# Gate stage of a two-block network: experts in products of 512 columns with halves added, half the low parts on GpSimd, one-hot rows by a comparison and a multiplication

## The reference

```python
top_s, top_pos = lax.top_k(cand_s, PEER_TOPK)
e = jnp.take_along_axis(cand_i, top_pos, axis=-1)
g = jax.nn.softmax(top_s, axis=-1).astype(xc.dtype)
a = jax.nn.gelu(jnp.einsum("td,thkd->thk", xc, w_down[e]))
return jnp.einsum("thk,thkd->td", g * a, w_up[e])
```

## Time and profile before

| | |
|---|---|
| median of 3 runs | 1985.24 us (1984.35 to 1985.85) |
| profiled execution, its own time | 1986.74 us |
| its span | 1984.9 us |
| TensorE busy | 1894.7 us, 95% |
| VectorE busy | 1416.2 us, 71% |
| ScalarE busy | 992.2 us, 50% |
| GpSimd busy | 257.3 us, 13% |
| chain that ended last | PE 77%, DVE 11%, ACT 3% |

### The profile page before, as it was taken

One profiled execution on the slowest core, in us unless ns is written; L12 is line 12 of the kernel. 1 busy time (PEld: TensorE's weight loads), 2 busy tenths in 40 slices (PEclk: granted clock), 3 DMA queues, 4 the chain that ended last, 5 costly groups with the idle time before them and its releaser, 6 DMA issues.

```text
span 1984.9 us, 32618 instructions
## 1 busy us (share of the span) xinstructions
PE 1894.7 (95%) x12858; PEld 1725.7 (87%) x12858; DVE 1416.2 (71%) x2574; ACT 992.2 (50%) x1442; POOL 257.3 (13%) x118
## 2 busy tenths in 40 slices
PE   6889899999988999999999899999999999999998
PEld 6887799999968799999998899999988888888886
DVE  5897775558957773338567559988878887777776
ACT  6555544455435554455555455566653334444444
POOL 0001044440001034430000066000000000000000
PEclk9999999999998999999999999999999999999999
DMA  8654477766564255545435354577766765555452
GB/s 323 240 191 142 150 246 255 265 213 204 179 230 141 109 182 190 191 170 197 166 132 170 108 172 167 181 216 216 219 211 251 301 236 227 194 219 205 171 206 112
DMA packets 94551, 391.92 MB, mean 197 GB/s; under 512 B 7680, under 2 KB 41776, under 8 KB 56000
## 3 DMA queue, kind: packets, MB, share of 16 engines
q1 hardware_dynamic: 94112, 389.58, 55.7%
q10 hardware_dynamic: 288, 0.26, 0.1%
HBM read 371.72 MB, written 15.73 MB: 195 GB/s over the span
## 4 chain that ended last, share of the span: by engine, by line
PE 77%; DVE 11%; ACT 3%; issue 2%; DMA 1%; POOL 0%; ACTq 0%; DVEq 0%; SPq 0%
PE acc L566 9%; PE acc L568 9%; PE acc L567 9%; PE ps L570 8%; PE ps L572 7%; PE ps L571 7%; PE ps L582 5%; PE acc L570 3%; PE acc L571 3%; PE acc L572 3%; PE ps L583 3%; DVE wlo L1361 2%; PE ps L1316 1%; PE acc L1316 1%; DVE arena L1390 1%
## 5 line engine op out<-in xcount | busy, mean ns | idle before, releaser
L2433 ACT ACTIVATE whi<-raw 128x1024 fp32r<-128x1024 f32 x557 | 588.4, 1059 | 443.0 <-PE acc L568 219.5
L1361 DVE TENSOR_TENSOR wlo<-raw,whi 128x1024 fp32r<-128x1024 f32 x461 | 569.5, 1242 | 309.1 <-ACT whi L2433 305.8
L570 PE MATMUL ps<-hpair,whi 128*128 128x256 f32 x1400 | 400.8, 286 | 7.2 <-DVE wlo L1361 3.4
L572 PE MATMUL ps<-hpair,wlo 128*128 128x256 f32 x1400 | 396.0, 283 | 0.0
L571 PE MATMUL ps<-hpair,whi 128*128 128x256 f32 x1400 | 396.0, 283 | 0.0
L1361 POOL TENSOR_TENSOR wlo<-raw,whi 128x1024 fp32r<-128x1024 f32 x96 | 239.9, 2502 | 616.0 <-ACT whi L2433 615.7
L566 PE MATMUL acc<-whi,chi 128*128 128x512 f32 x752 | 296.9, 395 | 3.5 <-DVE wlo L1361 1.9
L568 PE MATMUL acc<-wlo,chi 128*128 128x512 f32 x752 | 294.4, 391 | 0.0
L567 PE MATMUL acc<-whi,clo 128*128 128x512 f32 x752 | 293.9, 391 | 0.0
L570 PEld LDWEIGHTS ps<-hpair,whi 128*128 128x128 f32 x1400 | 268.4, 192 | 10.8 <-issue 4.1
L571 PEld LDWEIGHTS ps<-hpair,whi 128*128 128x128 f32 x1400 | 268.5, 192 | 0.6
(11 more groups left out here) (457 smaller groups left out, 2863.4 us busy)
## 6 DMA issues: line engine op xcount, KB each, us to landing
raw<-in_peer_down SPq DMA_DIRECT2D x64, 1024.0 KB, 4.9
raw<-in_peer_up SPq DMA_DIRECT2D x64, 1024.0 KB, 5.0
arena<-in_ada SPq DMA_DIRECT2D x80, 512.0 KB, 4.9
raw<-in_w_gate SPq DMA_DIRECT2D x22, 1024.0 KB, 4.7
raw<-in_w_up SPq DMA_DIRECT2D x22, 1024.0 KB, 4.8
raw<-in_w_down SPq DMA_DIRECT2D x22, 1024.0 KB, 4.8
arena<-spill SPq DMA_DIRECT2D x14, 1024.0 KB, 6.8
spill<-hT_t SPq DMA_DIRECT2D x22, 448.0 KB, 6.1
```

The source lines that it names most:

```text
L570: e.matmul(out, hi, xh, start=start, stop=False, skip_group_check=True)
L572: i = e.matmul(out, lo, xh, start=False, stop=stop, skip_group_check=True)
L1361: e.tensor_tensor(out=lo, in0=w, in1=hi.bitcast(F32), op=ALU.subtract).then_inc(*X(("lo", j)))
L2433: e.activation(hi, w, ACT.Copy, scale=1.0).then_inc(*self.A(("hi", j)))
```

## The change

1. Experts 21 to 71 use `pe_mm2`. VectorE adds the halves of expert i - 1 at the end of turn i, ScalarE takes their Gelu in place, behind the copies of the gate steps of turn i - 1. For expert 71 both stand in the expert stage.
2. The low parts of peer_down blocks 21 to 71 go to GpSimd where the number is odd and stay on VectorE where it is even.
3. The four instructions for `oh1` become a comparison of 512 columns (iota, repeated for four tokens, with the tokens' keys, each repeated 128 times) and, behind a wait for it, a multiplication in place by the gates, repeated likewise.

```diff
@@ lo_engine
+        if name == "peer_down" and STEP0 <= 2 * i + half < NST:
+            return ("V", "G")[half]
         if name[:5] == "peer_":
             return "V" if j >= self.block_no["peer_down", VLO0 // 2, VLO0 % 2] else "G"
@@ pe_expert_down
-        if i >= NST:
+        if i >= STEP0:
             for k in range(8):
                 self.pe_mm2(e, ps, self.W.tile(e, "peer_down", 8 * i + k), k, *([("full", "expert", i)] if k == 7 else []))
             return
@@ ve_gates
             for n in steps(i):
                 self.ve_one_hots(e, n)
             self.ve_cuts(e, "peer_down", 8 * i + 7)
+            if i > STEP0:
+                self.ve_expert_halves(e, i - 1)
@@ ve_one_hots
-        for i in range(4):
-            t = 4 * n + i
-            e.tensor_scalar(out=m.oh1[:, n % 3, i * 128:(i + 1) * 128], in0=m.iota, scalar1=m.pk[:, 0, t:t + 1],
-                            scalar2=m.pg[:, t:t + 1], op0=ALU.is_equal, op1=ALU.mult).then_inc(
-                                *V(*([("oh1", n)] if i == 3 else [])))
+        one = m.oh1[:, n % 3, :].rearrange("p (t n) -> p t n", t=4)
+        e.tensor_tensor(out=one, in0=bc(m.iota.unsqueeze(1), [128, 4, 128]),
+                        in1=bc(m.pk[:, 0, 4 * n:4 * n + 4].unsqueeze(2), [128, 4, 128]), op=ALU.is_equal).then_inc(*V())
+        e.wait_ge(*V.last)
+        e.tensor_tensor(out=one, in0=one, in1=bc(m.pg[:, 4 * n:4 * n + 4].unsqueeze(2), [128, 4, 128]), op=ALU.mult).then_inc(
+            *V(("oh1", n)))
@@ ve_experts
         self.ve_weigh(e, 0)
+        self.ve_expert_halves(e, NST - 1)
@@ se_gates
         for i in range(STEP0, NST):
-            self.se_expert_down(e, i)
-            for n in steps(i):
...
+            self.se_cuts(e, "peer_down", 8 * i + 7)
+            if i > STEP0:
+                for n in steps(i - 1):
+                    self.se_gates_out(e, n)
+                self.se_gelu(e, i - 1)
@@ se_experts
             if i + 1 >= NST and i < 127:
-                self.se_expert_down(e, i + 1)
+                self.se_cuts(e, "peer_down", 8 * (i + 1) + 7)
+                if i + 1 == NST:
+                    self.se_gelu(e, NST - 1)
+                self.se_gelu(e, i + 1)
```

More of the change, by code:

```diff
@@ L2972, in se_expert_down, with se_gelu, se_gates_out @@
         self.se_cuts(e, "peer_down", 8 * i + 7)
[L2973 to L2977, removed]
         e.wait_ge(*self.at("full", "expert", i))
-        if i == NPRE + 16:
-            e.wait_ge(*self.at("end", "picked", "P"))
         e.activation(m.ge_t[i], self.banks.tile("expert", i)[:, 0:T], ACT.Gelu_apprx_tanh, scale=1.0).then_inc(
             *self.A(("out", "expert", i), ("gelu", i)))
+    def se_gelu(self, e, i):
+        x = self.m.ge_t[i] if i < NST else self.m.co[:, i % 2, :]
+        e.wait_ge(*self.at("out", "expert", i))
+        e.activation(x, x, ACT.Gelu_apprx_tanh, scale=1.0).then_inc(*self.A(("gelu", i)))
     def se_gates(self, e):
-        m, A = self.m, self.A
         for i in range(STEP0, NST):
-            self.se_expert_down(e, i)
-            for n in steps(i):
[L2989 to L2996, removed]
+            self.se_cuts(e, "peer_down", 8 * i + 7)
[3 more added lines that the diff above has]
+                self.se_gelu(e, i - 1)
+    def se_gates_out(self, e, n):
+        m = self.m
+        k, c = n // 2 % 3, n // 6
+        st = m.stage[k].rearrange("p (n t) -> p n t", t=8)[:, :, 4 * (n % 2):4 * (n % 2) + 4]
+        e.wait_ge(*self.at("full", "gates", n))
+        if c and n % 2 == 0:
+            e.wait_ge(self.spilled[k], 16 * c)
+            e.wait_ge(self.kept, 16 * (n // 2 - 2))
+        e.activation(st.rearrange("p n t -> p t n"), self.banks.tile("gates", n)[:, :].rearrange("p (t n) -> p t n", t=4),
+                     ACT.Copy, scale=1.0).then_inc(*self.A(("out", "gates", n)))
     def se_experts(self, e):
```

## The result

The changed kernel takes **2021.12 us** (median of 5 runs, 2020.05 to 2022.99); the kernel before, run beside it, 1984.86 (5 runs, 1983.99 to 1985.85). The ratio is 1.0181, with a 95% interval of 1.0167 to 1.0195: slower by 36 us, where 2025 was forecast. The profiled execution took 2020.05 us, with a span of 2018.3 and a mean granted clock of 0.989.

A forecast was written before the change was run, and what follows sets the result against it. TensorE was taken to bound the stage, VectorE after the change: exclusion 36, way in 1.5 and 1, way out 0.4 less 0.2, Gelu 1.4, sum +40 on 1985.24 us, so 2025 us, range 2010 to 2042.

The forecast's parts named there:

- The bound and its exchange: Stretch 1262 to 1458 us: TensorE alone sets the pace before; after the change TensorE waits for VectorE's one-hot rows.
- Idle some 35 us: Sign in the new profile: TensorE idle that long between experts and gate steps, waiting for one-hot rows.
- The exclusion: Expert and gate-step stage: GpSimd's low parts and VectorE work with two SBUF sources exclude each other; +36 us (30 to 45).
- A step of VectorE: One gate step's one-hot work on VectorE: 1.97 us with the new pair, 0.34 more than 1.63; bounds 1.8 to 2.15.
- a hold: Each GpSimd low part adds some 2.3 us to VectorE's chain, less 0.65 if a reduction lies under it.
- A: Rival: the exclusion doesn't reach the one-hot instructions' repeated operands; -1.7 us, 1983.5 us; chance 0.09.
- B: Rival: no exclusion, but the one-hot pair is dearer, 2.15 us a step; +3 to +7, 1990 us; chance 0.04.
- C: Rival: no exclusion, and 512-column products go faster, 2.72 us an expert; -6, 1979 us; chance 0.03.
- The way in: Route's end and first gate step: block 21's low part on GpSimd costs 1.5 us, late first rows about 1.
- The way out: After the last gate steps: +0.4 us before expert 0's weighing, -0.2 for experts 69 to 71 without gate steps.
- Gelu 71: Expert stage: the later Gelu delays expert 71's weighing and peer_up 71's low part; +1.4 us once.
- Moved copies: ScalarE copies gate steps out of PSUM behind the next high part: costed at nothing, since no high part waits for a transfer.

The follow-up runs named there:

- fourth experiment: The changed kernel, with keys and gates of the one-hot operations read from the PSUM banks the transposes leave them in: 1986.1 us, ratio 1.0011.
- seventh: The kernel before with the one-hot pair (comparison and multiplication) alone: 1986.2 us, ratio 1.0005.
- eighth experiment: The kernel before with only the 512-column products, added halves and moved copies, Gelu of expert 71 taken early: 1982.55 us, ratio 0.9982.
- sixth: The kernel before with the one-hot pair and the odd low parts on GpSimd, old products: 2013.6 us, ratio 1.0143.
- tenth: The kernel before with one-hot pair, odd low parts on GpSimd, and ScalarE's gate copies moved behind the next expert's high parts: 1999.3 us, ratio 1.0069.
- fifth experiment: The kernel before with only the odd low parts of blocks 21 to 71 on GpSimd: 1991.8 us, ratio 1.0031.
- ninth experiment: The changed kernel with the low parts of experts 21 and 23 left on VectorE: 2017.9 us, ratio 1.0172.

## Why the prediction was right, and where its sizes were off

**The bound and its exchange: right.** TensorE set the pace before, VectorE does after, TensorE's idle time stands before the one-hot rows. "Idle some 35 us" was too much: the waits for one-hot rows are 22.6 us in the whole stage, and in the stretch of 196 us TensorE is idle for 196.00 - 176.19 = 19.8, or 2.8 per period of 27.8. The period is 3.8 over TensorE's 24.0; of the other 1.0, some 0.7 is work that the clock stretched (4.7 us in seven periods, below), and the rest is not taken apart.

**The exclusion: right in kind, oversized.** Forecast +36 (30 to 45), measured +26.9, which lies below the range; the period is 27.8, just under the 28.1 that was the lower bound. Three terms were each a little dear. A step of VectorE is 1.92 instead of 1.97, -0.4 per period. A reduction is 0.60 instead of 0.65, -0.3. And a hold was put at 2.3, with one reduction beside a low part "only by chance" (28.9 in the middle). In the trace a hold adds 2.17, because the held instruction's own 0.68 is work that was due anyway, and two of three low parts regularly begin ahead of a reduction: 5.4 for three instead of the 5.8 that 28.9 contained. That work which reads PSUM is not held rested on one row, 0.69 under GpSimd; the fourth experiment shows it for three lines of operations, 192 instructions in all, with GpSimd's low parts beside them.

**The rivals.** A said that repeated operands might not count: comparisons with two repeated sources took up to 2855 ns, so they do. The section of the Trainium skill named there ("SBUF — State Buffer", "SBUF: two separate sides"), by which A doesn't happen, agrees with the trace in this too. B had the price in the pair: a step is 1.92, not 2.15, and the fourth kernel, with pair and low parts, keeps to TensorE's 24.0. (That the pair alone costs nothing that can be measured, 1.0005 [0.9994, 1.0016] in the seventh, doesn't decide it: even at 2.15 a step VectorE's 24.0 would fit in 24.4 there.) C had faster long products: with a gate step at 0.89, as the prediction counts it, an expert takes 2.78 to 2.83 in the stage, where 2.81 was taken and C had 2.72.

**The way in: undersized.** 2.5 forecast, 5.7 measured. Of the two cases for the predicated copy, held or not, I took the middle, and the copy is held for full, 1.9. The first one-hot rows cost 2.5, not 1: I had counted the wait behind the low part of block 23 as mostly hidden. And 1.3 is the clock's, which no term had.

**The way out:** +0.4 - 0.2 forecast, 0.6 measured from the last gate steps to the first up product; then 1.4 more for the clock. **Gelu 71:** +1.4 forecast, +1.8 measured; the wait for the low part is 1.2, and the eighth experiment takes it away.

**Moved copies at nothing: right for a reason that I hadn't seen.** Their cover was named as nothing waiting for a transfer. What they do is keep the high parts from standing behind a copy that a held one-hot row makes late. Without the move (sixth against tenth, both with the old products) the holds cost 14 us more; with the new products no run lacks the move. I had costed the edit against the kernel before, in which there is no late row, and not against the one that the other edits make.

So the sum of 40 for a measured 36 was 9 too high in one term and 5.4 too low in the others. Its direction and its mechanism stand by experiment; its nearness is in part luck.

## What to carry to other kernels

Before work is moved to GpSimd, look where the sources of VectorE's instructions in that stage lie: here each low part of 2.4 us cost VectorE 1.6 to 2.2 us while all sources of the instruction it met were in SBUF, more than the 1.14 it took off, and nothing once one of two sources was read from PSUM. Two edits that each fit into an engine's slack (the pair 24.4, the low parts 24.4) need not fit together; sum them on the engine's own chain, and cost a moved instruction against the kernel that the other edits make. Where one engine is full for a whole stage, room on the others is worth nothing, however much of it an edit makes.

## What was not expected of the hardware

**TensorE's clock can fall after it has stood idle.** Stretches of the changed kernel (us; busy PE, PEld, DVE, ACT, POOL; granted clock, DMA share, GB/s):

```profile
1355.00:1360.00 5.00, 2.40 (x18) 2.10 (x17) 4.96 (x5) 1.13 (x2) 2.67 (x1) 1.00 0.53 137
1360.00:1365.00 5.00, 5.00 (x24) 4.50 (x24) 4.93 (x8) 3.76 (x5) 0.00 (x0) 0.66 0.83 284
```

TensorE's products there:

```profile
1359.75 1.75 PE L1318 MATMUL ps<-rs_t,arena 128*128 128x128 f32 x8 [2.60 <-DVE rs_t L2355]
1361.15 0.77 PE L584 MATMUL ps<-hpair,whi 128*128 128x512 f32 x1
1361.72 0.41 PE L585 MATMUL ps<-hpair,wlo 128*128 128x256 f32 x1
1361.94 0.63 PE L584 MATMUL ps<-hpair,whi 128*128 128x512 f32 x1
...
1364.05 0.40 PE L584 MATMUL ps<-hpair,whi 128*128 128x512 f32 x1
1364.28 0.28 PE L585 MATMUL ps<-hpair,wlo 128*128 128x256 f32 x1
```

After an idle 2.60 us a pair of products takes 0.64 from start to start (1361.94 to 1362.58), and from 1363.70 on 0.35: the engine ran at the lower of its two levels (1.2 GHz against 2.4), then at the full one again. That expert took 3.94 us instead of 2.86. TensorE stood idle for 2.2 to 3.0 us ten times from 1250 to 1500 us. Behind six of these gaps work ran at the lower level: expert 20 and those at 1267.58, 1332.34 and 1472.39 took 4.2 to 4.4 us, the one above 3.94, and the first up products took 1.4 more (expert 20 of the fifth experiment, behind 2.50, took 4.44). Behind the other four, which end at 1303.65, 1388.05, 1415.86 and 1443.68, the experts took their usual 2.86 to 2.90. One of these:

```profile
1415.86 1.13 PE L1318 MATMUL acc<-rs_t,arena 128*128 128x128 f32 x8 [2.92 <-DVE rs_t L2355]
1416.75 0.48 PE L584 MATMUL acc<-hpair,whi 128*128 128x512 f32 x1
```

and the stretch around it:

```profile
1415.00:1420.00 5.00, 4.14 (x28) 3.80 (x29) 4.97 (x9) 3.50 (x4) 0.00 (x0) 1.00 0.89 275
```

Its gap is longer than the one of 2.60 and the clock stayed at 1.00, so the length of a gap alone doesn't decide; what does isn't shown here. Inside the stage the lost time lies under VectorE's, which is later anyway. At the ends it is on the path: 1.3 us for expert 20, 1.4 for the first up products. The ninth experiment, without the idle gap, had no slow expert 20. So a wait on the full engine can cost half as much again as its own length.

**A longer pole may hide a loop.** That a hold of 2.2 us came back as 1.5 us more over ScalarE's queue (sixth and tenth) was not in any expectation of mine. It shows in no view of the kernel before, for there the loop has slack.
